# Expert layers: norm and routing merged into one stage, the weight stream begun in the stage ahead, and a nineteenth weight buffer

## The reference, cut to what matters

```python
x = x + gt1 * yl                                   # end of the mixer's projection
hl2 = rmsnorm(x, norm2_g[i]) * (1 + sc2) + sh2     # D = 1024
...
def hier_moe(h, w_grp, b_grp, w_exp, b_exp, w_gate, w_up, w_down):
    grp_logits = hf @ w_grp + b_grp                # 4 groups
    grp = jnp.argmax(grp_logits, axis=-1)
    exp_logits = (hf @ w_exp + b_exp)...           # 8 experts of the group
    top_logit, top_idx = lax.top_k(exp_logits, 2)
    ...
    # per expert, 32 of them: w_gate, w_up 1024 x 512, w_down 512 x 1024
    return (jax.nn.silu(xb @ w_gate[e]) * (xb @ w_up[e])) @ w_down[e]
```

## Time and profile before

| | |
|---|---|
| Time before, median of 3 runs | 3191.69 us (3189.46 to 3193.61) |
| Profiled execution: its time / its span | 3182.76 us / 3180.8 us |
| Mean granted TensorE clock | 0.948 |
| PE / PEld / DVE / ACT / POOL busy, share of the span | 85 / 62 / 34 / 16 / 10% |
| Moved by DMA | 638.61 MB, mean 201 GB/s |

### The profile page before, as it was taken

The page is one execution under the profiler, slowest core; times in us unless marked ns, Lnnn a source line. Parts: engine busy times, 40 slices in busy tenths (PEclk is TensorE's granted clock), DMA queues, the critical chain, the costliest instruction groups (busy, mean ns, idle before and its releaser), DMA issues. The chain is left out here.

```text
span 3180.8 us, 59082 instructions
## 1 busy us (share of the span) xinstructions
PE 2713.5 (85%) x25857; PEld 1969.9 (62%) x25857; DVE 1075.5 (34%) x2220; ACT 520.5 (16%) x1133; POOL 324.2 (10%) x358
## 2 busy tenths in 40 slices
PE   8999999989999977978776599798899977877775
PEld 7886766678868765444443244588888854444443
DVE  4563337435723222100001321565565422100002
ACT  1001132310011001000000100344444311000001
POOL 1000000000000002111110200232222202111110
PEclk9999999989999997999999799799999987999998
DMA  8684432157855128999998220000000029999994
GB/s 281 227 256 136 128 113 93 47 190 249 267 186 152 47 81 330 395 400 404 401 403 330 79 74 28 9 4 4 3 4 4 4 83 403 404 406 407 407 406 184
DMA packets 297239, 638.61 MB, mean 201 GB/s; under 512 B 29252, under 2 KB 198424, under 8 KB 262437
## 3 DMA queue, kind: packets, MB, share of 16 engines
q1 hardware_dynamic: 254896, 558.44, 47.9%
q10 hardware_dynamic: 30500, 61.96, 5.4%
q0 software_dynamic: 11600, 14.59, 1.4%
HBM read 634.79 MB, written 21.08 MB: 206 GB/s over the span
## 5 line engine op out<-in xcount | busy, mean ns | idle before, releaser
L2431 PE MATMUL bank<-expert_weights,ex_xt 128*64 128x256 f32 x2688 | 312.4, 388 | 92.3 <-DMA expert_weights<-in_moe_w_up_dram 80.0
L2431 PEld LDWEIGHTS bank<-expert_weights,ex_xt 128*64 128x64 f32 x2688 | 215.7, 140 | 203.8 <-issue 135.3
L533 PE MATMUL bank<-u,weights 128*128 128x272 f32 (+1 forms) x1408 | 318.3, 390 | 11.4 <-DVEq L556 11.4
L533 PEld LDWEIGHTS bank<-u,weights 128*128 128x128 f32 x1408 | 270.5, 192 | 59.0 <-DVEq L556 12.0
L2342 DVE TENSOR_TENSOR ex_hidden<-ex_silu,bank 128x256 f32<-128x256 f32 x64 | 27.0, 421 | 596.1 <-ACT ex_silu L2480 596.1
L1340 DVE SCALAR_TENSOR_TENSOR ada_acc<-ada_w,cond,ada_acc 128x512 f32 (+1 forms) x336 | 227.6, 746 | 1.6 <-PEq L505 1.6
L610 PE MATMUL bank<-rw_mixed,weights 128*128 128x512 f32 (+2 forms) x448 | 189.1, 583 | 31.7 <-DVEq L623 28.2
L2431 PE MATMUL bank<-weights,ex_xt 128*64 128x256 f32 x1408 | 168.3, 396 | 37.5 <-DMA weights<-in_moe_w_up_dram 36.1
L2452 PE MATMUL bank<-expert_weights,ex_hidden_turned 128*64 128x512 f32 x672 | 159.4, 618 | 21.7 <-DVE ex_hidden_turned L2345 21.7
L2431 PEld LDWEIGHTS bank<-weights,ex_xt 128*64 128x64 f32 x1408 | 113.5, 143 | 98.7 <-issue 60.9
L610 PEld LDWEIGHTS bank<-rw_mixed,weights 128*128 128x128 f32 (+1 forms) x448 | 84.0, 189 | 137.1 <-issue 135.3
(11 more groups left out here) (592 smaller groups left out, 4208.9 us busy)
## 6 DMA issues: line engine op xcount, KB each, us to landing
expert_weights<-in_moe_w_gate_dram SPq DMA_DIRECT2D x84, 1024.0 KB, 24.3
expert_weights<-in_moe_w_up_dram SPq DMA_DIRECT2D x84, 1024.0 KB, 24.6
expert_weights<-in_moe_w_down_dram SPq DMA_DIRECT2D x84, 1024.0 KB, 24.5
ada_w<-in_ada_w_dram ACTq DMA_DIRECT2D x24, 2048.0 KB, 9.3
weights<-in_moe_w_gate_dram SPq DMA_DIRECT2D x44, 1024.0 KB, 24.2
weights<-in_moe_w_up_dram SPq DMA_DIRECT2D x44, 1024.0 KB, 24.2
weights<-in_moe_w_down_dram SPq DMA_DIRECT2D x44, 1024.0 KB, 24.5
weights<-in_ga_w_in_dram SPq DMA_DIRECT2D x32, 1024.0 KB, 5.6
```

What stands on the lines that cost most here:

```text
L533: last = nc.tensor.matmul(k.bank[b + side * NB][:, 0:N], w[:, f, c * P:(c + 1) * P], rhs[:, f, 0:N], start=(f == 5), stop=(f == 4))
L2431: last = nc.tensor.matmul(half_cols(k.bank[2 + side], t), xt[:, s, f * SLOTS:(f + 1) * SLOTS], w[:, q * 512 + t * 256:q * 512 + t * 256 + ...
```

## The change

- **One stage.** `norm_stage` is no longer called for the experts; its work is part of `route_stage`. Chunk by chunk, VectorE scales both parts and, in layer 0, shifts the first; ScalarE shifts the other. TensorE accumulates the logits of all token tiles chunk by chunk, each as soon as the chunk is ready, in a bank of its own for each token tile; all transposes follow. The squares and the norm's scratch lie in ring slots 15 to 17, so pieces 15 and 16 wait for the sums and piece 17 for the scalings.
- **Shorter ranking.** Instead of a triangular of matmuls, VectorE adds up the earlier tiles' assignments (`fore`), and TensorE needs three matmuls for the places and one for the counts.
- **Gathers earlier.** POOL issues the gathers of experts 0 and 1 at the end of the route stage, as soon as the list is there and all row stores have landed, instead of at the start of the experts' stage.
- **Stream begun ahead.** `linear_stage` takes `behind`, which SP calls after each tile: the six pieces of expert 0 start in `gm_out` and `wo`, in stream buffers that their last tiles have left.
- **Nineteenth slot.** The ring has 19 slots; the last lies in `k.h`, whose tokens nobody needs any more but the staging rows, so piece 18 waits for the row stores. The refills follow the new count, and the overflow takes six slots that hold none of the two experts next in line.

The diff, cut to its core:

```diff
@@ class Stream: feed(..., behind=None)
             sp.wait_ge(used, (t // RING) * per_round + per_tile(t % RING))
             self.start_number(sp, seg.first + t + RING)
+            if behind is not None:
+                behind(sp, t)
@@ class ExpertRing
-    SLOTS = 18
+    SLOTS = 19
-    def begin(self, k):
-        self.slots, self.need = [s[:, 0:2048] for s in k.stream.slots], {}
+    def begin(self, k, a, l, seg, tiles):
+        first = seg.first + tiles
+        self.slots, self.need = [k.stream.slots[(first + j) % RING][:, 0:2048] for j in range(RING)], {}
+        def behind(sp, t):
+            if tiles > RING:
+                if t >= tiles - RING:
+                    self.start(sp, a, l, 0, t - (tiles - RING))
+            else:
+                for j in range(RING - tiles) if t == 0 else ():
+                    self.start(sp, a, l, 0, j)
+                self.start(sp, a, l, 0, RING - tiles + t)
+        return behind
...
-                for s in range(self.SLOTS - RING)]
-        self.slots += [s[:, :] for s in more]
+                for s in range(self.SLOTS - RING - 1)]
+        self.slots += [s[:, :] for s in more] + [k.h[:, :, :].rearrange("p c t -> p (c t)")[:, 0:2048]]
@@ class Route: load
-        k.ring.begin(k)
-        for j in range(k.ring.PIECES):
-            k.ring.start(sp, a, l, 0, j)
@@ route_stage: SP
+            route.load(sp)
             for e in range(1, 3):
-                for j in range(k.ring.PIECES):
-                    k.ring.start(sp, a, l, e, j)
+                for j in range(ring.PIECES):
+                    if ring.PIECES * e + j == 15:
+                        sp.wait_ge(summed, 1)
+                    if ring.PIECES * e + j == 17:
+                        sp.wait_ge(scaled, DC * len(parts))
+                    ring.start(sp, a, l, e, j)
+            for b in range(2):
+                sp.wait_ge(rstored[b], 16 * (TT // 2))
+            ring.start(sp, a, l, 3, 0)
@@ route_stage: POOL
+            pool.wait_ge(named, 1)
+            for b in range(2):
+                pool.wait_ge(rstored[b], 16 * (TT // 2))
+            for e in range(2):
+                gather(k, route, pool, e)
@@ route_stage: TensorE
-            for t in range(2):
-                turn(t)
+            for c in range(DC):
+                pe.wait_ge(squared, c + 1)
+                last = nc.tensor.matmul(k.bank[7][:, 0:T], k.ones[:, :], sq[c], start=(c == 0), stop=(c == DC - 1))
+            last.then_inc(summed, 1)
             pe.wait_ge(wl, 64)
-            for t in range(TT):
-                for f in range(DC):
-                    last = nc.tensor.matmul(k.bank[0][:, 64 * t:64 * t + NG + NE], hm[:, f, t * P:(t + 1) * P],
+            for f in range(DC):
+                if exact:
+                    pe.wait_ge(shifted, f + 1)
+                pe.wait_ge(ready, f + 1)
+                for t in range(TT):
+                    last = nc.tensor.matmul(k.bank[(0, 5, 6, 7)[t]][:, 0:NG + NE], hm[:, f, t * P:(t + 1) * P],
                                             wr[:, f, :], start=(f == 0), stop=(f == DC - 1))
             last.then_inc(made, 1)
-            for t in range(2, TT):
+            for t in range(TT):
                 turn(t)
...
+            nc.tensor.matmul(k.bank[5][:, 0:NE], before[:, :], A[:, 0, :], start=True, stop=True)
+            nc.tensor.matmul(k.bank[5][:, NE:NE * TT], before[:, :], flat_of(A[:, 1:TT, :]), start=True, stop=False)
+            pe.wait_ge(assigned, TT)
+            nc.tensor.matmul(k.bank[5][:, NE:NE * TT], k.ones[:, :], flat_of(fore[:, 0:TT - 1, :]), start=False, stop=True)
@@ route_stage: ScalarE
+            for c in range(DC):
+                t0, t1, _, shift = parts[exact]
+                act.wait_ge(scaled, len(parts) * c + exact + 1)
+                nc.scalar.activation(hm[:, c, t0:t1], hm[:, c, t0:t1], ACT.Identity, bias=shift[:, c:c + 1])
@@ route_stage: VectorE
+            for c in range(DC):
+                for t0, t1, gain, _ in parts:
+                    nc.vector.scalar_tensor_tensor(out=hm[:, c, t0:t1], in0=k.x[:, c, t0:t1], scalar=gain[:, c:c + 1],
+                                                   in1=rr[:, t0:t1], op0=ALU.mult, op1=ALU.mult).then_inc(scaled, 1)
+                if exact:
+                    t0, t1, _, shift = parts[0]
+                    dve.wait_ge(scaled, len(parts) * c + 1)
+                    nc.vector.tensor_scalar(hm[:, c, t0:t1], hm[:, c, t0:t1], shift[:, c:c + 1], None, ALU.add)
...
+            nc.vector.tensor_copy(fore[:, 0, :], A[:, 0, :]).then_inc(assigned, 1)
+            for t in range(1, TT):
+                dve.wait_ge(assigned, t + 1)
+                nc.vector.tensor_tensor(fore[:, t, :], fore[:, t - 1, :], A[:, t, :], ALU.add).then_inc(assigned, 1)
@@ experts_stage: SP
-            for e in range(3, NE):
+            for n in range(ring.SLOTS, NE * ring.PIECES):
+                e, j = divmod(n, ring.PIECES)
+                if n == (AFTER + 3) * ring.PIECES:
...
+                done, part = divmod(n - ring.SLOTS, ring.PIECES)
+                sp.wait_ge(spent, 4 * done + (1, 1, 2, 2, 3, 4)[part])
+                ring.start(sp, k.a, l, e, j)
@@ moe
-        norm_stage(k, f"moe_norm{l}", k.x, DC, D, EPS, parts, hm, loads=route.load)
         k.ring.place(k, more)
-        route_stage(k, route, hm)
+        route_stage(k, route, hm, parts)
```

More of the change, by code:

```diff
@@ L1838, in gmlp @@
             linear_stage(k, "gm_out", seg["ga_out"], whole_tiles(GC, P), None, TB, write, 6,
-                         first=gate_bias, halves=[(0, SEQ, lambda f: u[:, f, :]), (SEQ, TB, lambda f: gated_ctx[:, f, :])])
+                         first=gate_bias, behind=k.ring.begin(k, a, 0, seg["ga_out"], 8),
+                         halves=[(0, SEQ, lambda f: u[:, f, :]), (SEQ, TB, lambda f: gated_ctx[:, f, :])])
 def gmlp_v_stage(k, h, v, mods, tables, tables_landed, spatial):
@@ L2110, in route_stage @@
         nobody = sb("nobody", [P, SLOTS, 4], I32)
+        fore = sb("fore", [P, TT, NE])
+        T, ring = route.T, k.ring
+        per = 2048 // T
+        sq = [ring.slots[15 + c // per][:, c % per * T:c % per * T + T] for c in range(DC)]
+        r0, mean, rr = (ring.slots[17][:, n * T:(n + 1) * T] for n in range(3))
+        exact = 1 if l == 0 else 0
+        squared, summed, meaned, rooted, scaled, shifted, ready, named = (k.sem(f"rt_{n}") for n in (
+            "squared", "summed", "meaned", "rooted", "scaled", "shifted", "ready", "named"))
         names = ("made", "vdone", "exped", "gmaxed", "assigned", "placed", "rturned", "rcopied", "rstored0",
@@ L2235, in _ @@
             dve.wait_ge(made, 1)
-            link(nc.vector.tensor_tensor(
-                L[:, :, :], k.bank[0][:, 0:64 * TT].rearrange("p (t n) -> p t n", n=64)[:, :, 0:NG + NE],
-                bias[:, :].unsqueeze(1).broadcast_to([P, TT, NG + NE]), ALU.add))
+            for t in range(TT):
+                last = nc.vector.tensor_tensor(L[:, t, :], k.bank[(0, 5, 6, 7)[t]][:, 0:NG + NE], bias[:, :], ALU.add)
+            link(last)
             link(nc.vector.tensor_reduce(route.stat(2), L[:, :, 0:NG], AX.X, ALU.max))
@@ L2283, in _ @@
             dve.wait_ge(inverted, 1)
-            nc.vector.tensor_scalar(route.tokens[:, :], k.bank[7][0:SLOTS, 0:NE], float(NOBODY), None, ALU.add)
+            nc.vector.tensor_scalar(route.tokens[:, :], k.bank[7][0:SLOTS, 0:NE], float(NOBODY), None, ALU.add)\
+                .then_inc(named, 1)
             dve.wait_ge(inverted, 2)
@@ L2288, in _, with gather @@
             dve.wait_ge(exped, TT + 1)
+def gather(k, route, pool, e):
+    pool.indirect_dma_start(route.xg[:, e % 2, :], None, route.rows,
+                            bass.IndirectOffsetOnAxis(ap=route.tokens[0:SLOTS, e:e + 1], axis=0),
+                            bounds_check=route.T - 1, oob_is_err=False).then_inc(k.ring.got[e % 2], 16)
 def experts_stage(k, route):
@@ L2505, in __init__ @@
         self.k, self.nc, self.route = k, k.nc, route
-        self.w = k.ring.slots[RING:RING + 6]
+        held = [n % k.ring.SLOTS for n in range((self.AFTER + 1) * k.ring.PIECES, (self.AFTER + 3) * k.ring.PIECES)]
+        self.w = [slot for s, slot in enumerate(k.ring.slots) if s not in held][:6]
         self.xg, self.xt, self.act_out, self.hid, self.y, self.listed = xg, xt, act_out, hid, y, listed
@@ L2821, in write @@
                                                   in1=k.x[:, m, 0:SEQ], op0=ALU.mult, op1=ALU.add)
-        linear_stage(k, "wo", seg["wo"], whole_tiles(DC, 256), lambda f: gate[:, f, :], SEQ, write, 4)
+        linear_stage(k, "wo", seg["wo"], whole_tiles(DC, 256), lambda f: gate[:, f, :], SEQ, write, 4,
+                     behind=k.ring.begin(k, a, 1, seg["wo"], 4))
 LEVELS = 6
```

67 lines of the change are left out of this document (36 added, 31 removed).

## The result

The changed kernel takes 3174.7 us (median of 5 runs, 3168.6 to 3176.7) against 3191.0 us: 0.9947 of the time before, 95% interval 0.9935 to 0.9959. It is faster by 0.5%, 16.3 us, where 24.7 us were forecast.

What follows compares the result with a forecast made beforehand. The weight stream of the two expert layers was taken to set the pace; 13.6 us in layer 0 plus 11.1 in layer 1 made 24.7, from the median 3191.69 to 3167 us; own range 3161 to 3175, 8-in-10 range 3159 to 3180.

Steps and rivals of the forecast that it cites:

- rival (a): Row stores between logits and gather take the gain: layer 0 4.8, layer 1 some 9; 14 us, 3178; chance 0.18.
- signs of being wrong: Gather waits for the list, TensorE for the boundary, stores over 10 us, or a piece over 2.8 us.
- Logits: Routing: layer 0's 64 narrow matmuls take 12.6 us and end at 1197.6; layer 1's logits end at 2628.7.
- Stores: Token rows before the gather: layer 0's first lands in 8 us, layer 1's second in 8.8 us.
- rival (b): Row stores land fast, 2.7 to 5 us each: layer 0 gains some 18, layer 1 some 15; 3159; chance 0.09.
- The boundary: End of layer 0's routing stage passes while gathers 0 and 1 fly, ending at 1222.5, before TensorE begins at 1223.4.
- Piece 18 beside the gather: Layer 0, gather to transposes: piece 18 flying beside costs between nothing and 2.78 us, taken as 0.5.
- The slot: Nineteenth ring slot: one piece more in by the first refill, 2.78 us in layer 0, 2.70 in layer 1.
- Layer 1: Second expert layer: refill issued at 2658.5, streaming 8.4 us earlier, plus 2.70 for the slot; 11.1 us gained.
- Early stream: Expert 0's six pieces started in the stage ahead cost nothing in gm_out; without that, layer 0's stores wait six times 2.78 us.

Runs made afterwards that it cites:

- e9: e7 with eighteen weight buffers, so in layer 0 only piece 17 is issued behind the gathers; 3159.8 us, ratio 0.9906.
- e7: e5, but in layer 0 pieces 17 and 18 are issued when gathers 0 and 1 have landed; 3159.5 us, ratio 0.9904.
- e4: Changed kernel with expert 0's six pieces issued at the routing stage's start instead of in the stage ahead; 3186.9 us, ratio 0.9986.
- e8: Changed kernel with the norm a stage of its own again, ahead of routing; 3192.8 us, ratio 1.0009.
- e10: Changed kernel keeping only the merged stage: expert 0's pieces issued in it, eighteen slots, gathers behind the boundary; 3181.9 us, ratio 0.9968.
- e2: Changed kernel without POOL's drain at the routing stage's end and without the clearing of semaphores behind it; 3163.4 us, ratio 0.9924.
- e1: Changed kernel with gathers 0 and 1 issued behind the stage boundary again; 3168.7 us, ratio 0.9937.
- e3: Changed kernel with eighteen weight buffers instead of nineteen; 3173.3 us, ratio 0.9953.
- e5: e2 with late tiles staged in buffer 17 (layer 0) and pieces from the twelfth held for both stores (layer 1); 3166.6 us, ratio 0.9945.
- e6: e5 with eighteen weight buffers, none in the first path's token memory; 3169.7 us, ratio 0.9938.

## Why the prediction was right, and where its steps failed

Sign and range were right, the range just so: 3174.7 us lies at the upper end of the forecast's own 3161 to 3175, nearer to rival (a)'s 3178 than to 3167. The chain that was to set the pace does: logits, stores, gather, transposes, refill, with a drain between the last two that the forecast didn't have. Two of the prediction's own signs of being wrong came true: TensorE waits for the boundary, and a store takes over 10 us. The 16.3 us lie between the forecast's 24.7 and rival (a)'s 14, and the layers' 14.1 us are (a)'s sum, though not its split (9.1 and 5.0 where (a) had 4.8 and 9).

*Logits.* Forecast 1197.6, that is 26.1 us after the layer's start; read at 29.4. The sums ran 1.7 us slower than before, at the lower clock (not the change's: e9, which runs e7's code up to there, has 7.1 us where e7 has 8.8), and the 64 narrow matmuls took 13.8 us, the slow bound, not 12.6. In layer 1 forecast 14.8, read at 15.4.

*Stores.* In layer 0 the first landed within 6.6 us (8 forecast) and the gather went 46.7 us after the start (44.5 forecast), late by less than the logits. In layer 1 the second took 10.7 us instead of 8.8, which was the median of before's two, 8.1 and 9.5 (issued 2630.88, and SP's piece 18, which waits for it, went at 2641.60), and the gather went at 32.1 (29.0 forecast). The stream beside it decides this (e4, e8, e10). Beside rival (b) stood the rule in the Trainium skill, "DMA: Bandwidth & Descriptors", section "Queues, rings and completion order", that an engine goes round its queues by packets. The trace agrees with the rule, but not with the estimate of under 5 us that I made from it. SP's queue (q1) keeps the engines to itself until 2632.46, 3.9 us after the first store's issue at 2628.56; from then on ScalarE's (q10) has packet for packet with it, of fewer bytes each. Why the first packet comes so late isn't shown; with idle engines it came 0.8 us after the issue (layer 0's third store). Queues of after from 2628.5 to 2632.4 and from 2633 to 2637:

```profile
q1 hardware_dynamic: 378, 1.48, 100.6%
```
```profile
q1 hardware_dynamic: 158, 1.08, 64.6%
q10 hardware_dynamic: 159, 0.59, 36.4%
```

*The boundary.* This is the step that failed: "The boundary now passes while they fly". It doesn't: POOL's drain holds it until both gathers are in (6.2 and 8.4 us; 0.13 without gathers in flight). With the clearing it cost 1.9 and 2.5 us at TensorE's start and 3.2 and 5.0 us at the layers' ends (e2); the surplus goes with the earlier `places` and scatters, which I didn't separate. The early issue was to save the boundary's 4.4 us; by the traces the kernel is faster without it (e1). That layer 0's 7.5 us from gather to transposes all the same match the forecast's 7.4 (6.9 and 0.5) is luck. The 6.9 us were read in before, where the stream had not run dry when the gather went out: SP's queue moved 1.88 MB from 1227.4 to 1234.2. In after it had, but for piece 18, and the drain took what that saved; without it the gather took 5.5 us (e2). So in layer 0 the forecast was missed at the logits, the stores and the slot.

```profile
q1 hardware_dynamic: 487, 1.88, 71.1%
```

*Piece 18 beside the gather.* "I take 0.5" was too little: 1.6 us of drain in layer 0 (e3), and 2.0 to 3.0 us a piece without the drain (e5 to e7). The same page of the Trainium skill, section "SWDGE vs HWDGE vs iDMA", says that GpSimd's and the other DMAs use different queues inside each engine, which takes turns between them; by that I would estimate a fraction of a piece. The measured gathers came later by about a piece's full time, and the measurement decides; the turns are in the trace (e5's second stretch), but they begin only with the gather's late first packet.

*The slot.* 2.78 + 2.70 us was mis-sized by all of it, as far as these traces can tell. Shown: its piece delays the gather and so the refill (3.2 us in layer 0, e5 against e6). In layer 1 a slot more makes between 1.8 and -2.6 us, where two traces of the same code already differ by 1.7. Not shown: why it brings nothing in layer 0 of e7 either. The scatters go out there from 1229.75 to 1238.75, across the refill at 1232.40, and in that stretch DMA moved only 279 GB/s with its engines fully busy (last columns); I didn't separate what that cost.

```profile
1230.00:1236.00 6.00, 6.00 (x56) 3.73 (x53) 0.00 (x0) 0.14 (x1) 4.68 (x5) 0.97 1.01 279
```

*Layer 1.* The first refill came 0.3 us earlier, not 5.5: 3.0 us were lost up to the gather, most of it at the stores, and 2.2 at the drain. Most of the gain of 5.0 us is, by this reckoning, the backlog: before, 4.3 us of pieces were still queued at the refill, after, none (the windows above).

*Early stream.* The six pieces were to "cost nothing" in the stage ahead, and by the medians they bring 12 us (e4; 11.3 by the traces): the stores' free way in layer 0, the start of the stream in layer 1. The parts don't add up. Without the early stream e4 gains 4 us, without the merged norm e8 nothing, the merged norm alone 9; together 16. The two that gain less each carry the early gathers with their drain, the third doesn't. I read it so, without a run that shows it alone: each part shortens the chain only where the stores don't meet the stream.

## What to carry to other kernels

Before you move an asynchronous transfer ahead of a stage boundary, look in the boundary's source line for drains: GpSimd's gathers in flight were waited for there, by every engine, and what stood behind the boundary started later. SP's pieces were not: its drain took 0.12 us with piece 18 in flight. When a small transfer sits on the critical chain of a streaming kernel, hold the bulk pieces that would be issued just ahead of it, and let them go when it has landed; here that (e7), with the drain and the clearing removed and the stores' way cleared, gave 0.9904 where the change gave 0.9947. Don't count one more buffer as one piece's price: here it brought nothing that the runs could tell, with its piece in front of the gathers or behind them.

## What was unexpected of the hardware

POOL's drain took 0.13 us with no gather of its own in flight and 4.6 to 9.0 us with two (e3 in layer 0, e8 in layer 1), longer when the DMA engines had more to move beside them. A gather of 64 rows took 3.65 us from issue to TensorE's use with idle DMA engines, 5.6 and 8.6 us behind one and two 1 MiB transfers of another queue. A 512 KB store took 2.6 us alone and 10.7 us in a full stream, where its queue's first packet moved 3.9 us after the first issue.
